# A two-block network on one core: gating branch of the first mixing taken out of its tail, two orders swapped in linear attention, and pooling's subtraction moved into the matrix products

## The reference

```python
# first mixing (block 1, layer 0): linear recurrence beside a gated branch
u = jax.nn.gelu(u)
v = rmsnorm(jax.nn.gelu(v).reshape(B, S, 4, 128), gmlp_v_norm.reshape(4, 128))
w_causal = gmlp_w_s * jnp.tril(jnp.ones((128, 128)))
sv = jnp.einsum('gts,bnsgd->bntgd', w_causal, v.reshape(B, nc, 128, 4, 128)) + gmlp_b_s.T[:, :, None]
out_b = u * sv.reshape(B, S, B_W)
out_a = rmsnorm(hgrn2_recurrence(q, k, v_a, log_f), hgrn_out_norm) * jax.nn.silu(og)

# linear attention (block 2, layer 0), forwards and backwards over chunks of 64
att = where(lower, q_t @ k_t.T, 0);  o = att @ v + q_t @ S;  S = decay * S + k_end.T @ v

# pooling (block 2, layer 1): windows of 2, 4, 8, 16 tokens, one for each 256 features
pooled = (total / count - h).astype(h.dtype)
y = jnp.einsum('btgc,gce->btge', pooled, w_pool) * pool_scale
```

## Time and profile before

| | us |
|---|---|
| median of 3 runs | 3181.8 |
| lowest and highest of these | 3168.32 and 3184.36 |
| the profiled execution, its own time | 3158.51 |
| its span in the trace | 3156.8 |

### The profile page before, as it was taken

The page is one execution under the profiler, slowest core; times in us unless marked ns, Lnnn a source line. Parts: engine busy times, 40 slices in busy tenths (PEclk is TensorE's granted clock), DMA queues, the critical chain, the costliest instruction groups (busy, mean ns, idle before and its releaser), DMA issues. The chain is left out here.

```text
span 3156.8 us, 66323 instructions
## 1 busy us (share of the span) xinstructions
PE 3089.9 (98%) x25784; PEld 3022.7 (96%) x25784; DVE 2159.0 (68%) x3611; ACT 1577.8 (50%) x2733; POOL 284.1 (9%) x194
## 2 busy tenths in 40 slices
PE   9899999999999899999999999999999899999998
PEld 9699999999999799999999999999997799999898
DVE  4559888889997559898878887333255455555654
ACT  5264566655554655576655555222245344454443
POOL 0116300000001006400000000000020010000100
PEclk9899999999998999999999999999999799999999
DMA  5156644478896256644479896333342146555464
GB/s 185 61 158 195 197 146 142 150 256 290 287 353 232 82 158 192 195 152 140 145 258 316 310 318 202 95 98 96 97 116 73 41 152 192 175 189 184 135 193 145
DMA packets 172779, 560.64 MB, mean 178 GB/s; under 512 B 22480, under 2 KB 31440, under 8 KB 172000
## 3 DMA queue, kind: packets, MB, share of 16 engines
q1 hardware_dynamic: 172640, 558.82, 54.4%
HBM read 557.71 MB, written 1.05 MB: 177 GB/s over the span
## 5 line engine op out<-in xcount | busy, mean ns | idle before, releaser
L236 ACT ACTIVATE peer_e_hi<-raw 128x1024 fp32r<-128x1024 f32 x560 | 590.5, 1055 | 376.9 <-PE peer_e_out L1503 307.9
L240 DVE TENSOR_TENSOR peer_e_lo<-raw,peer_e_hi 128x1024 fp32r<-128x1024 f32 x498 | 611.0, 1227 | 176.5 <-ACT peer_e_hi L236 172.1
L240 DVE TENSOR_TENSOR ffn_lo<-raw,ffn_hi 128x1024 fp32r<-128x1024 f32 x256 | 312.9, 1225 | 458.2 <-ACT ffn_hi L236 458.2
L236 ACT ACTIVATE ffn_hi<-raw 128x1024 fp32r<-128x1024 f32 x264 | 279.5, 1062 | 520.4 <-PE ffn_acc L2766 328.6
L1499 PE MATMUL peer_e_out<-x_normed,peer_e_hi 128*128 128x256 f32 x2048 | 493.7, 283 | 0.0
L1500 PE MATMUL peer_e_out<-x_normed,peer_e_hi 128*128 128x256 f32 x2048 | 482.3, 278 | 0.0
L1565 PE MATMUL peer_e_out<-peer_h_pair,peer_e_hi 128*128 128x256 f32 x2048 | 477.8, 276 | 0.4 <-DVE peer_e_lo L240 0.4
L1566 PE MATMUL peer_e_out<-peer_h_pair,peer_e_hi 128*128 128x256 f32 x2048 | 477.7, 276 | 0.0
L1500 PEld LDWEIGHTS peer_e_out<-x_normed,peer_e_hi 128*128 128x128 f32 x2048 | 385.9, 188 | 0.0
L1499 PEld LDWEIGHTS peer_e_out<-x_normed,peer_e_hi 128*128 128x128 f32 x2048 | 385.7, 188 | 0.0
L1565 PEld LDWEIGHTS peer_e_out<-peer_h_pair,peer_e_hi 128*128 128x128 f32 x2048 | 384.5, 188 | 0.7 <-issue 0.7
(11 more groups left out here) (635 smaller groups left out, 6018.8 us busy)
## 6 DMA issues: line engine op xcount, KB each, us to landing
raw<-in_l_down SPq DMA_DIRECT2D x256, 512.0 KB, 3.6
raw<-in_l_up SPq DMA_DIRECT2D x256, 512.0 KB, 4.8
raw<-in_ffn_wi SPq DMA_DIRECT2D x176, 512.0 KB, 3.8
peer_e_ring<-in_w_mod SPq DMA_DIRECT2D x144, 512.0 KB, 5.2
raw<-in_ffn_wo SPq DMA_DIRECT2D x88, 512.0 KB, 3.7
raw<-in_l_peer_w_query SPq DMA_DIRECT2D x32, 512.0 KB, 3.6
raw<-in_w_in SPq DMA_DIRECT2D x26, 512.0 KB, 3.8
l_in_raw<-in_l_w_in SPq DMA_DIRECT2D x24, 512.0 KB, 4.4
```

Source lines behind the costliest of these rows:

```text
L236: return act.activation(hi, v, ACT.Copy)
L240: return eng.tensor_tensor(lo, v, hi.bitcast(F32), ALU.subtract)
```

## The change

The first mixing: the squares of `gv` are summed on ACT as they are made (eight instructions with an accumulator instead of one), root and scale follow on ACT, with a small inverse on DVE before step 3. The eight products with the causal weights stand on PE in the place of `keep_awake` after steps 5, 6 and 7 and, the last two, after the turned scores; they go to `o_ps`. ACT takes them from there with the gain as scale, and DVE adds the bias and multiplies by `u` right after the last `pick`. The products of one row are gone. PE waits for ACT's taking before it writes `o_ps`.

Linear attention: DVE runs the carried state of the context first and masks the scores after that; on PE `score(1)` stands ahead of `carried(0)`.

Pooling: DVE makes only the scaled value; ACT adds the shift (L3483 of the changed kernel) and makes the negative of the same value (`less`, L3486). PE multiplies `less` and then `pooled` with the weights into the same sums. `pool_inv` is loaded ahead of `w_pool`, and `keep_awake` has 14 products instead of 40.

```diff
@@ first mixing, DVE
+                if i == 3:
+                    gmlp.vector_invert(dve)
...
-            gmlp.vector_norm(dve)
+            gmlp.vector_gate(dve)
...
-            gmlp.vector_gate(dve, gmlp_ps)
@@ first mixing, PE
                 mm.then_inc(product, 1)
-                keep_awake(pe, K, l_ps[:, 0, 0:P], 2)
+                if i < HC - 3:
+                    keep_awake(pe, K, l_ps[:, 0, 0:P], 2)
+                else:
+                    gmlp.tensor(pe, o_ps, 2 * (i - HC + 3), 2 * (i - HC + 4))
...
             mm.then_inc(turned, 1)
+            gmlp.tensor(pe, o_ps, 6, 8)
...
             pe.wait_ge(picked, LEVELS + 1)
+            pe.wait_ge(gmlp.taken, 1)
...
             head_norms.tensor_sums(pe)
-            gmlp.tensor(pe, gmlp_ps)
             head_norms.tensor_spread(pe)
@@ first mixing, ACT
             gmlp.scalar_squares(act)
+            gmlp.scalar_scale(act)
...
+            gmlp.scalar_take(act, o_ps)
             act.wait_ge(leveled, LEVELS + 1)
             act.activation(att_last[:], last_ps, ACT.Copy).then_inc(across, 1)
-            gmlp.scalar_root(act)
@@ Gmlp
     def scalar_squares(self, act):
-        act.activation(self.sq[:], self.g4, ACT.Square).then_inc(self.squared, 1)
+        waste = self.sq[:].rearrange("p g (n d) -> p (g n) d", d=P)
+        for i in range(TT * self.GROUPS):
+            ins = act.activation(waste[:, i], self.g4[:, i], ACT.Square, accum_out=self.ss[:, i:i + 1])
+        ins.then_inc(self.squared, 1)
+        act.wait_ge(self.squared, 1)
         act.activation(self.root[:], self.ss[:], ACT.Sqrt, bias=self.K.eps[:], scale=1.0 / P).then_inc(self.rooted, 1)
+    def vector_invert(self, dve):
         dve.wait_ge(self.rooted, 1)
+        dve.reciprocal(self.rstd[:], self.root[:]).then_inc(self.inverted, 1)
+
+    def scalar_scale(self, act):
+        act.wait_ge(self.inverted, 1)
+        for i in range(TT * self.GROUPS):
+            ins = act.activation(self.g4[:, i], self.g4[:, i], ACT.Copy, scale=self.rstd[:, i:i + 1])
+        ins.then_inc(self.scaled, 1)
+
+    def scalar_take(self, act, acc):
+        act.wait_ge(self.mixed, 1)
+        gain = self.K.col("l0_gmlp_v_norm")
         for g in range(self.GROUPS):
+            ins = act.activation(self.sq[:, g], acc[:, g], ACT.Copy, scale=gain[:, g:g + 1])
+        ins.then_inc(self.taken, 1)
+
+    def vector_gate(self, dve):
...
+        dve.wait_ge(self.taken, 1)
+        dve.tensor_tensor(by_tile, by_tile, bias, ALU.add).then_inc(self.biased, 1)
+        dve.wait_ge(self.biased, 1)
+        dve.tensor_tensor(self.mix[:, 4:8], self.sq[:], self.u[:], ALU.mult)
@@ linear attention, DVE
-                dve.wait_ge(scored, d + 1)
-                dve.copy_predicated(att.rearrange("p a b t i -> p (a b t) i"),
...
                 chain(dve.memset(carry, 0.0))
+                dve.wait_ge(summed, d + 1)
...
                         if s == 0 and i == 0:
+                            dve.wait_ge(scored, d + 1)
+                            dve.copy_predicated(att.rearrange("p a b t i -> p (a b t) i"),
@@ linear attention, PE
             def score(d):
+                pe.wait_ge(copied, d + 1)
...
             add(1)
+            score(1)
             carried(0)
-            score(1)
             own(1)
@@ pooling
+            sp.dma_start(inv[:], dram["pool_inv"].partition_broadcast(P)).then_inc(inv_in, 16)
             sp.dma_start(w[:], dram["w_pool"].rearrange("g (c p) e -> p g c e", p=P)).then_inc(w_in, 16)
-            sp.dma_start(inv[:], dram["pool_inv"].partition_broadcast(P)).then_inc(inv_in, 16)
...
-            norm.vector_to(dve, DC)
-            dve.wait_ge(norm.done_v, DC)
-            dve.wait_ge(inv_in, 16)
+            norm.vector_scale(dve, DC)
+            dve.wait_ge(normed, DC)
...
-                dve.tensor_tensor(pooled[:, cs], pooled[:, cs], h[:, cs], ALU.subtract).then_inc(ready, 1)
...
-            norm.tensor(pe, acc[:, 0, 0:P], 40)
+            norm.tensor(pe, acc[:, 0, 0:P], 14)
             pe.wait_ge(w_in, 16)
             for g in range(4):
+                pe.wait_ge(turned, 2 * g + 3)
+                products(g, less, True)
+            for g in range(4):
                 pe.wait_ge(ready, g + 1)
+                products(g, pooled, False).then_inc(product, 1)
...
+            for c in range(DC):
+                act.wait_ge(norm.scaled, c + 1)
+                act.activation(h[:, c], norm.sq[:, c], ACT.Identity, bias=norm.shift[:, c:c + 1]).then_inc(normed, 1)
+            act.wait_ge(turned, 1)
+            for c in range(DC):
+                act.activation(less[:, c], norm.sq[:, c], ACT.Identity, bias=less_shift[:, c:c + 1], scale=-1.0)\
+                    .then_inc(turned, 1)
```

More of the change, by code:

```diff
@@ L3379, in pool_mix @@
     with stage(nc, "pool") as st:
-        w_in, inv_in, cleared, v_step, product, ready = (
-            st.sem(x) for x in ("w_in", "inv_in", "cleared", "v_step", "product", "ready"))
+        w_in, inv_in, cleared, v_step, product, ready, normed, turned = (
+            st.sem(x) for x in ("w_in", "inv_in", "cleared", "v_step", "product", "ready", "normed", "turned"))
         w = st.sb("w", [P, 4, 2, T])
@@ L3386, in pool_mix @@
         pooled = st.sb("pooled", [P, DC, T])
+        less = st.sb("less", [P, DC, T])
+        less_shift = st.sb("less_shift", [P, DC])
         acc = st.ps("acc", [P, DC, T])
@@ L3437, in _, with products @@
         def _(pe):
[L3438 removed]
+            def products(g, x, first):
+                for j in range(2):
+                    for c in range(2):
+                        mm = pe.matmul(acc[:, 2 * g + j], w[:, g, c, j * P:(j + 1) * P], x[:, 2 * g + c],
+                                       start=first and j == c == 0, stop=not first and c == 1, skip_group_check=True)
+                return mm
+            norm.tensor(pe, acc[:, 0, 0:P], 14)
             pe.wait_ge(w_in, 16)
             for g in range(4):
+                pe.wait_ge(turned, 2 * g + 3)
+                products(g, less, True)
+            for g in range(4):
                 pe.wait_ge(ready, g + 1)
[L3442 to L3446 removed]
+                products(g, pooled, False).then_inc(product, 1)
             for c in range(DC):
@@ L3452, in _ @@
             act.activation(norm.primed[:], K.eps[:], ACT.Sqrt)
+            act.activation(less_shift[:], norm.shift, ACT.Copy, scale=-1.0).then_inc(turned, 1)
+            for c in range(DC):
[5 more added lines that the diff above has]
+                    .then_inc(turned, 1)
+            act.wait_ge(turned, DC + 1)
             for c in range(DC):
```

61 lines of the change are left out of this document (24 added, 37 removed).

## The result

The changed kernel took 3148.1 us in the median of 20 runs beside 3168.5 us for the kernel before (20 runs each): ratio 0.9942, interval 0.9921 to 0.9962, so 18.4 us faster (12 to 25); the two medians lie 20.4 us apart. A second comparison gave 0.9923 (0.9890 to 0.9956). The profiled execution took 3153.8 us, its span was 3152.1.

A forecast was written before the change was run, and what follows sets the result against it. PE was the first suspect in the three stages, with DVE ending last in the pooling. First mixing -9.8, linear attention -3.1 and pooling +0.4 gave -12.5 us, from 3181.8 to 3169.3, range 3155 to 3179.

The forecast's parts named there:

- The base: Whole kernel: the starting time was taken as the median 3181.8 us, 23 us above the profiled execution.
- Linear attention: Linear attention: both new orders were to save 3.1 us, with ends -1 and -6.
- The three pauses: Linear attention: PE's waits for DVE of 0.41, 1.38 and 1.34 us were all to vanish.
- The upper end of 6: Linear attention: 6 us won if PE, no longer pausing, gets back to 2.4 GHz in the last part.
- First mixing: First mixing: the spread starts 10.0 us earlier, the inverse costs 0.2, sum -9.8 us (ends -7 and -13).
- that rival: First mixing: slower squares make the root late for DVE's step 3, 2 us back, 3171.3; chance 0.08.
- I leave it at 3.78: First mixing: the spread's 16 records still take 3.78 us; staying at 2.4 GHz would win 1.7 more.
- Pooling: Pooling: root 1.0 us earlier, a clock fall costing 1.4, together +0.4 us (ends -2.9 and +1.8).
- the row behind 116.77: First mixing: after 2.56 us idle, 32 records took 5.44 us for 4.1; used to price the pooling's fall at 1.4.
- The swap: Linear attention rival: the swap does nothing as the later mask delays `own(1)`, 3.1 us back, 3172.4; chance 0.08.
- the cold pooling: Pooling rival: PE stays at 1.2 GHz, +2.1 us, 3183.9, deciding from about 55 slow records; chance 0.04.
- The clock is kind: Rival, four places in first mixing and pooling (-1.7, -1.4, -1.4, -1.9): three give 17.2 us won, 3164.6; chance 0.25.

The follow-up runs named there:

- gla_swap: The kernel before with only PE's order changed in linear attention, `score(1)` ahead of `carried(0)`, DVE's order old: ratio 0.9964 (0.9930 to 0.9999).
- gla_fill: The kernel before with DVE's new order in linear attention, PE's order old, plus eight identity products between `add(1)` and `carried(0)`: stage 92.6 us, 98.4 before.
- pool_only: The kernel before with only the pooling's part of the change: ratio 1.0007 (0.9983 to 1.0031), root 23.6 us after the stage's start.
- all_w_first: The changed kernel with the pooling's weights loaded ahead of the counts: root 22.3 us after the stage's start, 28.1 in the changed kernel; timed later at 0.9923.
- changed_again: The changed kernel run once more, unaltered, against the kernel before: ratio 0.9923 (0.9890 to 0.9956), median 3152.9 us.

## Why the prediction was off, step by step

**The base.** "Taken from the median, 23 us above that execution" took 3181.8, the median of three runs, as the kernel's time. Twenty runs gave 3168.5. This is 13.3 of the 21.2 us between forecast and result; the profiled execution with 3158.5 had been a hint that three runs lay high.

**Linear attention, the term that was mis-sized.** This is the step that failed. "Sum 0.41 + 1.38 + 1.34 = -3.1 us (ends -1 and -6)". The three pauses went as worked out, each of them, and the mask was early enough. But the step took the clock as it was. From the first mask's end to the end of the last carried part the time went from 27.5 to 18.1 us: 3.1 by the pauses, 1.7 by the second own part, 2.9 by the second carried part, and 1.8 by the scores and the first carried part together. In the mean of the profiles the stage went from 99.2 (five with both old orders) to 88.7 (eleven with both new ones), -10.5, and this stretch from 29.0 to 17.8. The upper end of 6 had the clock come back in the last part only, through the pauses. The runs show another cause: the clock fell ahead of the pauses, in or just behind the first carried part, and the second scores moved ahead of it (gla_swap), or sixteen dummy records merely added (gla_fill), hold it up. The range of 3155 was missed by this and the base together; either alone would have stayed inside. A time more than 0.5% below the base had been given 0.35. (Two sums of the prediction are off by a little and change nothing: `own(1)` ends at 2496.0 + 3.78 = 2499.8, and 64 records of 0.23 us are 14.7.)

**First mixing, right.** Forecast -9.8 us with the spread at 3.78; the mean went from 55.6 (eight profiles) to 44.3 (eleven), -11.3. The squares cost 0.29 to 0.31 us each and overlapped their readings, so they ended at 91.1 and the root was 3.4 us ahead of its reader: that rival fell. The spread took 2.05 us in four of eleven profiles and 2.5 to 3.8 in the others, so "I leave it at 3.78" is the upper end of what occurs. The changed kernel itself had 43.8 us once and 47.0 the other time. The Trainium skill ("TensorE: Matmul & The Clock Gate", "What's actually happening") says that the point at which the clock changes isn't tied to the kernel's start and differs from run to run; these two profiles of one kernel agree.

**Pooling: the direction of the risk right, the size off.** +0.4 was forecast, with ends -2.9 and +1.8; the root came 2.6 and 2.4 us later than in the earlier trace rows with the whole change and 1.9 earlier in pool_only (against 24.9, the mean of nine profiles with the old pooling, 3.2 and 3.0 later and 1.3 earlier). The weights landed 8.8 us after the stage's start for 8.1 forecast, and the fall of the clock cost 10.20 - 7.14 = 3.1 us for 1.4 forecast: the row behind 116.77 had a fall that ended sooner (0.50 from 118 to 120 us and 0.94 from 120 to 122; in the pooling 0.50 from 2934 to 2938). The turned order of the loads was costed as a later landing, but never questioned: the counts could come second, as all_w_first shows, and it was the turned order that made both the wait and the fall. The Trainium skill's rule on gaps (same page, "Why this matters for your kernels") would have let all of these pass: here 2.75 and 2.60 us ended in a fall, 1.29 and 0.24 didn't, and 2.12 in the first mixing went both ways.

**The rivals.** The swap did something, the cold pooling stayed at about 32 slow records at most, below its point of decision. "The clock is kind" was the nearest case, and its size (17.2 us) was right by luck. Of its four places the two in the first mixing came out so in the changed kernel's profile (spread 2.05, level records 3.90), though not in changed_again (3.64, 5.43). The two in the pooling went the other way in both: the gap cost 3.1 us and the weights were late. Linear attention, with most of the missing time, wasn't in it.

## What to carry to other kernels

Where a stage runs at half clock, price a reordering of PE by what it does to the clock as well as by the waits: look for the window in which the clock falls and at what PE does there, even when PE isn't idle. When work is moved onto an engine that waits for a load, ask anew which of the loads has to be first. And take the base of a small forecast from many runs: three scattered by 16 us here, and a single unchanged stage can be 375 or 389 us long.

## What the hardware did that was not expected

- The clock fell with PE busy throughout: windows of 2.00 us busy out of 2.00 at 0.63 and 0.67, in a run of products with 64 rows and 64 columns. Sixteen dummy records (2.05 us) earlier in PE's order prevented it and paid for themselves.
- Products of one row between large ones cost about 0.5 us a record at a granted clock of 0.50; eight of them (16 records) were 8 us.
- Two transfers issued 0.4 us apart: the weights (1 MB) landed after 5.6 to 5.9 us when first and 7.0 to 8.4 when second, the counts (512 KB) after 3.6 to 4.2 and 6.9 to 7.9.
- Long unchanged stages took one of two lengths, 6 to 15 us apart, in nearly every profile. In changed_again four unchanged stages took the longer one at once (30.6, 391.0, 195.8 and 195.7 us for 24.4, 375, 189 and 189) and the execution took 3174.8 us where the lowest of its kernel in that comparison was 3135.3. Why was not tried.
